# Turning a small side input on VectorE instead of TensorE, in the middle of a feed-forward stage

## The chip, the cores and the metric

The kernel runs on one core of one Trainium2 chip. The metric is the device time of one execution in microseconds (us), the smaller the better. TensorE is written PE, VectorE DVE, ScalarE ACT, GpSimd POOL, SyncE SP. PEld is TensorE's weight load.

## The reference, cut to what matters

Two transformer blocks run one after the other on one sequence of 256 rows with model width 1024, all in float32. The first block ends with a relu-squared feed-forward and a gate fed by the small side input `p` (256 x 256):

```python
h2 = rms_norm(x, g_mlp[i])
x = x + jnp.square(jax.nn.relu(h2 @ w_ff1[i])) @ w_ff2[i]     # 1024 -> 4096 -> 1024

gate_p = jax.nn.sigmoid(rms_norm(x, g_ple[i]) @ w_ple_gate[i])
x = x + gate_p * (p[i] @ w_ple[i])                            # p: 256 x 256, w_ple: 256 x 1024
```

The second block (two gated feed-forwards around an attention stage) follows.

## The kernel before, in words

**Split products.** Each float32 operand is held as a high part (a copy rounded to the type `fp32r`) and a low part (the operand minus its high part). A product is three matmuls: high by high, high by low, low by high. Both weights and activations are split so.

**Units.** The weights come in as *units* of 128 x 2048, in a fixed order written out by hand. SP loads a unit into one of six `raw` buffers, ACT copies it to `w_hi` (line 1034, four buffers; it waits until the unit four before is used up), and DVE subtracts to `w_lo` (`lo`, line 1479), in place of `raw`. For a few units POOL does this subtraction (line 2159). PE waits, at the start of each unit, for `lo_ready` to have counted that unit (`products`, matmuls in line 519). In this stage a unit is 24 matmuls of 512 columns.

**The relu stage.** The width 4096 is cut into eight slices, i = 0 to 7. With ff the number of the stage's first unit, slice i takes two units for the way up (for i > 0, ff+4(i-1) and the one after; slice 1 takes ff+2 and ff+3) and two for the way down. PE's order is up(i), then down(i-2). So for i = 5 PE works on units ff+16 and ff+17 (up), then ff+18 and ff+19 (down of slice 3). For each slice:

- ACT takes the relu of the two PSUM banks into `act_r` (line 1212), DVE makes the square into `act_f` (`square`, line 1740) and frees the banks,
- DVE turns `act_f` into `relu_T` with 16 transposes of 32 x 256 (`relu_turn`, line 1755), which wait for both squares to be finished,
- ACT copies the high part to `fT_hi` or `fE_hi` (line 1216), DVE subtracts the low part (`relu_low`, line 1762).

DVE's order in slice i > 2 is `lo(v+3)`, `relu_low(i-1)`, `lo(v+4)`, the two squares, `relu_turn(i)`, `lo(v+5)`, `lo(v+6)`, with v = ff+4(i-1). All queues run in the order of the program.

**The side input.** POOL loads `p` into `p_sb` ahead of the stage (line 2201). After up(0), PE turns it with four transposes (matmuls with the unit matrix, line 533) into one PSUM bank of the two *work* banks (6 and 7), which serve all such turned batches of the kernel in turn, by each batch's number in one list (`WB`). ACT then copies the bank to `pT_hi` (line 1041) and DVE subtracts to `pT_lo` (line 1498), between the second square and `relu_turn(0)`. The product with `w_ple` uses them at the end of the stage (`ple_product`).

**The idle buffer.** `act_T` (128 x 512) holds turned activations in the two gated feed-forwards of the second block. They fill it with the same sort of 16 transposes, of 32 x 128 (line 1848). In the relu stage it is not used.

Of the kernel before, what the change touches and what calls it, by code (L numbers as in the profile page):

```python
# [28 lines left out]
P = 128  # L29
D, TB, SEQ = 1024, 2, 256  # L30
# [66 lines left out]
def work_batches():  # L97

    order = [("mix", 0, 0), ("mix", 1, 0), ("mix", 0, 1), ("mix", 1, 1)]
    for k in range(IN_CB):  # L100
        if 6 <= k < 14:
            order += [("v", k - 6)]
        if k == IN_CB - 1:
            order += [("ya", 0, 0)]
        if 12 <= k:
            order += [("rv", k - 12)]
    order += [("ya", 0, 1)]
    order += [("ya", 1, h) for h in range(2)]
    order += [("yr", tb, h) for tb in range(TB) for h in range(2)]
    order += [("m", tb, h) for tb in range(TB) for h in range(2)]  # L110
    order += [("mlp", tb, h) for tb in range(TB) for h in range(2)]
    order += [("p",)]
    order += [("ple", tb, h) for tb in range(TB) for h in range(2)]
    order += [("ffn1", tb, h) for tb in range(TB) for h in range(2)]
    order += [("mix2", tb, h) for tb in range(TB) for h in range(2)]
    order += [("cq", 0), ("cq", 1), ("ckv",)]
    for kind in "bl":
        for j in range(BH // 2):
            order += [(kind + "a", 2 * j), (kind + "a", 2 * j + 1)]
            order += [(kind + "v", j)]  # L120
    order += [("ffn2", tb, h) for tb in range(TB) for h in range(2)]
    return {name: n for n, name in enumerate(order)}
# [56 lines left out]
def two_blocks(nc, x_d, p_d, g_mix, w_in, lam_q1, lam_k1, lam_q2, lam_k2, g_diff, g_ret, w_bd, w_br, w_out,  # L179
# [3 lines left out]
    f32, f32r, bf16, i32 = mybir.dt.float32, mybir.dt.float32r, mybir.dt.bfloat16, mybir.dt.int32  # L183
    ALU, ACT = mybir.AluOpType, mybir.ActivationFunctionType
# [51 lines left out]
    def lay(start, *parts):  # L236

        out = []
        for name, shape, *dt in parts:
            out.append(sb(name, shape, dt[0] if dt else f32, start))  # L240
            start += -(-4 * int(np.prod(shape[1:])) // 32) * 32
        assert start <= nc.sbuf_usable_end, (name, start)
        return out
# [15 lines left out]
    fT0, fT1, act_r, act_f, pl_s, sg, pT0, pT1, p_sb, gain_mid, fE0, fE1 = lay(  # L259
        arena, ("fT_hi", [P, 4, SEQ], f32r), ("fT_lo", [P, 4, SEQ], f32r), ("act_r", [P, TB, HALF]),  # L260
        ("act_f", [P, TB, HALF]), ("pl_s", [P, TB, D]), ("sg", [P, TB, D]),
        ("pT_hi", [P, 2, SEQ], f32r), ("pT_lo", [P, 2, SEQ], f32r), ("p_sb", [P, TB, 256]), ("gain_mid", [P, D]),
        ("fE_hi", [P, 4, SEQ], f32r), ("fE_lo", [P, 4, SEQ], f32r))
    fT, pT, fE = [fT0, fT1], [pT0, pT1], [fE0, fE1]
    act_T, relu_T = lay(named["fE_lo"] + 16 * SEQ, ("act_T", [P, 2, SEQ]), ("relu_T", [P, 4, SEQ]))
# [34 lines left out]
    def sem(name):  # L300
        sems[name] = ctx.enter_context(nc.semaphore(name))
        return sems[name]
# [10 lines left out]
    p_in, ident_in, mask_in, lam_in, gd_in = (sem(n) for n in ("p_in", "ident_in", "mask_in", "lam_in", "gd_in"))  # L313
# [15 lines left out]
    proj_done, proj_out = sem("proj_done"), sem("proj_out")  # L329
    qk_turned = sem("qk_turned")  # L330
    acc_done, acc_out = sem("acc_done"), sem("acc_out")
    relu_turned, f_hi, f_ready = sem("relu_turned"), sem("f_hi"), sem("f_ready")
    act_turned, turned_hi, turned_lo = sem("act_turned"), sem("turned_hi"), sem("turned_lo")
    up_done, act_ready, up_out = sem("up_done"), sem("act_ready"), sem("up_out")
# [162 lines left out]
    def _(pe):  # L497
# [25 lines left out]
        def work_free(n, dw=0):  # L523
            if n >= 2:
                pe.wait_ge(work_out[n % 2], n // 2 + dw)

        def turn(name, blocks, dw=0):

            work_free(WB[name], dw)
            col = 0  # L530
            for blk in blocks:
                rows, cols = blk.shape[0], blk.shape[-1]
                mm = pe.transpose(work(name)[0:cols, col:col + rows], blk, ident)  # L533
                col += rows
            mm.then_inc(work_done, 1)

        def turned(name, dw=0):
            n = WB[name]
            pe.wait_ge(work_out[n % 2], n // 2 + 1 + dw)
# [203 lines left out]
        def ff_up0(u0, norm):  # L743

            out = [up(0, 0)[:, :]]
            products(out, hA, 0, 4, 0, u0, HALF, True, False, operand=norm)
            turn_rows(norm, x, 1, (0,))
            products(out, hA, 4, 2, 0, u0 + 1, HALF, False, False, operand=norm)
            turn_rows(norm, x, 1, (1,))
            products(out, hA, 4, 4, 0, u0 + 1, HALF, False, True, t0=2, operand=norm).then_inc(up_done, 1)  # L750
            narrow_block(up(1, 0)[:, :], norm, u0, 1, HALF)
# [13 lines left out]

        u = U0["ff"]
        ff_up0(u, "mlp")
        pe.wait_ge(p_in, 16)
        turn(("p",), [p_sb[:, tb, k * P:(k + 1) * P] for k in range(2) for tb in range(TB)])

        def relu_up(i):

# [32 lines left out]
        def ple_product(tb):  # L805

            if tb:
                pe.wait_ge(pl_out, 1)
            turned(("p",))
            mm = products([bank[4 + c][:, :] for c in range(2)], pT, 0, 2, tb, U0["pl"], D, True, True)  # L810
            mm.then_inc(unit_used if tb else pl_done, 1)

# [208 lines left out]
    def _(act):  # L1021
        def loads(u):

            return 32 * (u // RAW_SLOTS + (u % RAW_SLOTS > 1))

        def hi(u, turns=0):

            if u >= N_UNITS:
                return
            if u >= HI_SLOTS:  # L1030
                act.wait_ge(unit_used, u - HI_SLOTS + 1 + 12 * turns)
            act.wait_ge(raw_in[u % RAW_SLOTS], loads(u) + 64 * turns)
            w = unit_width(u)
            act.activation(w_hi[u % HI_SLOTS][:, 0:w], raw[u % RAW_SLOTS][:, 0:w], ACT.Copy).then_inc(hi_ready, 1)  # L1034

        def split(name, di=0):

            act.wait_ge(work_done, WB[name] + 1 + 2 * di)
            (dst, _), b = rows_of(name)
            if name[0] not in COLUMN:  # L1040
                act.activation(dst, b, ACT.Copy).then_inc(split_hi, 1)
                return
            c0 = COLUMN[name[0]] + BLOCKS * name[2]
            act.wait_ge(g_ready, 1 if name[0] == "mix" else 2)
            for n in range(BLOCKS):
                act.activation(dst[:, n, :], b[:, n, :], ACT.Copy, scale=g_col[:, c0 + n:c0 + n + 1]).then_inc(split_hi, 1)  # L1046
# [171 lines left out]
        relu(0, 0)  # L1218
        hi(U0["ff"] + 4)
        relu(0, 1)  # L1220
        split(("p",))

        hi(U0["ff"] + 5)
        relu_split(0)
# [4 lines left out]
        for i in range(2, DFF // HALF):  # L1229
            v = U0["ff"] + 4 * (i - 1)  # L1230
            hi(v + 3)
            relu_split(i - 1)
            hi(v + 4)
            for tb in range(TB):
                relu(i, tb)
            hi(v + 5)
            hi(v + 6)
# [122 lines left out]
        for n in range(1, 5):  # L1360
# [6 lines left out]
            if n == 2:  # L1367
                act.wait_ge(proj_out, copies(CB_IN2 + 2))
                for tb in range(TB):
                    for m, (buf, cols) in enumerate(((cq, QR), (ckv, KVR))):  # L1370
                        if tb or m:
                            act.wait_ge(csq, 2 * tb + m)
                        k = 2 * m + tb
# [41 lines left out]
        for tb in range(TB):  # L1415
            k = act.activation(k_tm[:, tb, :, NOPE:MQ], kr[:, tb, :].unsqueeze(1).to_broadcast([P, MH, ROPE]), ACT.Copy)
# [47 lines left out]
    def _(vec):  # L1464
# [26 lines left out]
        def split(name, di=0):  # L1491

            if name[0] in COLUMN:
                low_blocks(name, range(BLOCKS))
                return
            (hi, dst), b = rows_of(name)
            vec.wait_ge(split_hi, SPLIT[name] + 1 + 2 * di)
            vec.tensor_tensor(dst, b, hi.bitcast(f32), ALU.subtract).then_inc(work_out[WB[name] % 2], 1)
# [244 lines left out]
        square(0, 0)  # L1743
        lo(U0["ff"] + 4)
        square(0, 1)
        split(("p",))

        def relu_turn(i):

            vec.wait_ge(up_out, 2 * i + 2)  # L1750
            whole = act_f[:, :, :].rearrange("p t (k j f) -> p t k j f", j=4, f=32)
            there = relu_T[:, :, :].rearrange("p k (t a c) -> p t k a c", a=4, c=32)
            for a in range(4):
                for j in range(4):
                    t = vec.transpose(there[32 * j:32 * j + 32, :, :, a, :], whole[32 * a:32 * a + 32, :, :, j, :])  # L1755
            t.then_inc(relu_turned, 1)

        def relu_low(i):

# [12 lines left out]
        for i in range(2, DFF // HALF):  # L1772
            v = U0["ff"] + 4 * (i - 1)
            if i > 2:
                lo(v + 3)
            relu_low(i - 1)
            if i > 2:
                lo(v + 4)
            for tb in range(TB):
                square(i, tb)  # L1780
            if i == 2:
                vec.wait_ge(lo_ready, v + 5)
                lo(v + 5)
            relu_turn(i)
            if i > 2:
                lo(v + 5)
            lo(v + 6)
# [524 lines left out]
```

## Time and profile before

| | |
|---|---|
| median of 3 runs | 966.04 us (965.82 to 966.35) |
| the profiled execution: its own time | 966.08 us |
| its span, first to last instruction | 964.2 us |
| the relu stage in that span | from about 283 to 451 us |

The span counts from the first instruction of the profile. An execution's own time is the span and 1.9 us around it. Starts in the rows below are in us from the span's start; a row of a timeline may hold several instructions one after the other.

### The profile page before, as it was taken

What the parts mean: (1) busy time and instruction counts of PE and PEld (TensorE: products, weight loads), DVE (VectorE), ACT (ScalarE), POOL (GpSimd) and SP (SyncE); (2) the same over time, 40 slices, a digit from 0 to 9 for tenths busy, and PEclk for the clock granted to TensorE, in tenths of its full rate; (3) what the DMA queues carried; (4) which work ended last, traced back from release to release, by engine and by line L of the source; (5) the groups of instructions that cost most, each with busy time, mean ns of one, the idle gap of its engine ahead of it and who ended that gap; (6) DMA issues with size and microseconds to landing.
All of it is one profiled execution on the core that took longest, in us unless ns stands there. A gap on an engine that the chain in (4) does not pass through costs nothing.

```text
span 964.2 us, 12923 instructions
## 1 busy us (share of the span) xinstructions
PE 956.4 (99%) x4468; PEld 786.7 (82%) x4468; DVE 772.1 (80%) x1489; ACT 500.9 (52%) x666; POOL 162.5 (17%) x118
## 2 busy tenths in 40 slices
PE   9999999999999999999999999999999999999997
PEld 6887778888888888888888888888887788888886
DVE  6897997578669799884778987877878878887875
ACT  7545556644463644444765444444648665444442
POOL 3552444310013300000133000000133023000000
PEclk9999999999999999999999999999999999999999
DMA  9865555434455755554566656553654255656531
GB/s 343 269 193 167 165 174 175 150 130 175 175 203 205 240 176 191 202 187 164 172 215 196 213 177 204 187 177 113 223 182 147 88 175 187 206 177 206 184 131 44
DMA packets 98725, 175.67 MB, mean 182 GB/s; under 512 B 5920, under 2 KB 54128, under 8 KB 98672
## 3 DMA queue, kind: packets, MB, share of 16 engines
q1 hardware_dynamic: 97024, 171.53, 53.0%
q0 software_dynamic: 1344, 3.19, 1.2%
q8 instruction: 31, 0.51, 0.2%
q10 hardware_dynamic: 304, 0.27, 0.1%
q14 instruction: 22, 0.18, 0.1%
HBM read 173.91 MB, written 1.05 MB: 181 GB/s over the span
## 4 chain that ended last, share of the span: by engine, by line
PE 93%; DVE 4%; issue 1%; ACT 1%; POOL 1%; DMA 0%; POOLq 0%; ACTq 0%; DVEq 0%
PE bank L519 86%; PE bank L533 2%; DVE relu_T L1755 2%; DVE w_lo L1479 1%; PE bank L578 1%; PE bank L577 1%; PE bank L904 1%; PE bank L589 1%; POOL w_lo L2159 0%; ACT w_hi L1034 0%; PE bank L960 0%; DMA g_rows<-in_g_mix 0%; PE bank L591 0%; PE bank L590 0%; DVE act_f L1740 0%
## 5 line engine op out<-in xcount | busy, mean ns | idle before, releaser
L519 PE MATMUL bank<-w_hi,hA 128*128 128x512 f32 (+1 forms) x1752 | 544.8, 390 | 0.0
L1034 ACT ACTIVATE w_hi<-raw 128x2048 fp32r<-128x2048 f32 (+1 forms) x162 | 305.8, 1893 | 196.7 <-PE bank L519 194.9
L519 PEld LDWEIGHTS bank<-w_hi,hA 128*128 128x128 f32 x1752 | 327.4, 188 | 67.7 <-issue 1.1
L1479 DVE TENSOR_TENSOR w_lo<-raw,w_hi 128x2048 fp32r<-128x2048 f32 (+1 forms) x138 | 308.2, 2254 | 63.1 <-ACT w_hi L1034 58.1
L519 PE MATMUL bank<-w_lo,hA 128*128 128x512 f32 (+1 forms) x876 | 334.3, 388 | 0.0
L519 PEld LDWEIGHTS bank<-w_lo,hA 128*128 128x128 f32 x876 | 164.5, 188 | 33.0
L2159 POOL TENSOR_TENSOR w_lo<-raw,w_hi 128x2048 fp32r<-128x2048 f32 x21 | 96.8, 4609 | 154.5 <-ACT w_hi L1034 121.9
L1848 DVE STREAM_TRANSPOSE act_T<-act_f 32x128 f32<-32x128 f32 x352 | 106.5, 303 | 5.7 <-DVE act_f L1836 0.7
L2145 POOL TENSOR_SCALAR ms<-ss 128x1 f32<-128x1 f32 x15 | 9.8, 654 | 515.9 <-ACT junk L1064 515.6
L519 PE MATMUL bank<-w_hi,fT_hi 128*128 128x512 f32 x232 | 71.5, 389 | 0.0
L519 PE MATMUL bank<-w_hi,fT_lo 128*128 128x512 f32 x232 | 71.4, 389 | 0.0
L519 PE MATMUL bank<-w_lo,fT_hi 128*128 128x512 f32 x232 | 71.4, 389 | 0.0
L1755 DVE STREAM_TRANSPOSE relu_T<-act_f 32x256 f32<-32x256 f32 x128 | 55.8, 436 | 1.9
L519 PEld LDWEIGHTS bank<-w_lo,fT_hi 128*128 128x128 f32 x232 | 43.5, 188 | 9.0
L519 PEld LDWEIGHTS bank<-w_hi,fT_lo 128*128 128x128 f32 x232 | 43.5, 188 | 9.0
L519 PEld LDWEIGHTS bank<-w_hi,fT_hi 128*128 128x128 f32 x232 | 43.5, 188 | 9.0
L1290 ACT ACTIVATE act_r<-bank,rs 128x256 f32<-128x256 f32 x44 | 20.6, 474 | 54.0 <-PE bank L519 52.2
L1506 DVE SCALAR_TENSOR_TENSOR hA<-bank,g_col,hA 128x128 fp32r<-128x128 f32 x92 | 25.3, 344 | 15.6 <-ACT hA L1046 15.4
L1836 DVE SCALAR_TENSOR_TENSOR act_f<-bank,rs,act_r 128x256 f32<-128x256 f32 x44 | 20.8, 480 | 21.2 <-ACT act_r L1290 21.1
L1575 DVE STREAM_TRANSPOSE aT<-L 32x96 f32<-32x96 f32 x128 | 34.5, 270 | 1.9
L1046 ACT ACTIVATE hA<-bank,g_col 128x128 fp32r<-128x128 f32 x92 | 25.5, 378 | 18.2 <-PE bank L533 18.1
L519 PE MATMUL bank<-w_hi,hB_hi 128*128 128x512 f32 x96 | 30.4, 398 | 0.0
(281 smaller groups left out, 906.7 us busy)
## 6 DMA issues: line engine op xcount, KB each, us to landing
raw<-in_w_in SPq DMA_DIRECT2D x74, 512.0 KB, 4.7
raw<-in_w_ff SPq DMA_DIRECT2D x64, 512.0 KB, 4.0
raw<-in_ffn_w_gate SPq DMA_DIRECT2D x44, 512.0 KB, 3.9
raw<-in_ffn_w_up SPq DMA_DIRECT2D x44, 512.0 KB, 4.8
raw<-in_ffn_w_down SPq DMA_DIRECT2D x44, 512.0 KB, 4.0
raw<-in_w_out SPq DMA_DIRECT2D x16, 512.0 KB, 3.8
raw<-in_w_branch_diff SPq DMA_DIRECT2D x8, 512.0 KB, 3.9
raw<-in_w_branch_ret SPq DMA_DIRECT2D x8, 512.0 KB, 3.7
```

What stands on the lines that cost most here:

```text
L519: mm = pe.matmul(o, a, w, start=first and t == 0 and m < len(outs), stop=last and t == n - 1 and m >= len(todo) - len(outs))
L533: mm = pe.transpose(work(name)[0:cols, col:col + rows], blk, ident)
L1034: act.activation(w_hi[u % HI_SLOTS][:, 0:w], raw[u % RAW_SLOTS][:, 0:w], ACT.Copy).then_inc(hi_ready, 1)
L1046: act.activation(dst[:, n, :], b[:, n, :], ACT.Copy, scale=g_col[:, c0 + n:c0 + n + 1]).then_inc(split_hi, 1)
L1290: act.activation(act_r[:, tb, 0:SUB], up(tb, i)[:, 0:SUB], ACT.Silu, scale=inv_rms(norm, tb))\
L1479: vec.tensor_tensor(w_lo[u % RAW_SLOTS][:, 0:w], raw[u % RAW_SLOTS][:, 0:w], w_hi[u % HI_SLOTS][:, 0:w].bitcast(f32), ALU.subtract).then_i ...
L1506: vec.scalar_tensor_tensor(out=dst[:, n, :], in0=b[:, n, :], scalar=g_col[:, c0 + n:c0 + n + 1], in1=hi[:, n, :].bitcast(f32), op0=ALU.mul ...
L1575: t = vec.transpose(there[32 * j:32 * j + 32, :, a, :], whole[32 * a:32 * a + 32, :, j, :])
L1755: t = vec.transpose(there[32 * j:32 * j + 32, :, :, a, :], whole[32 * a:32 * a + 32, :, :, j, :])
L1836: vec.scalar_tensor_tensor(out=act_f[:, tb, 0:SUB], in0=up(tb, i)[:, SUB:2 * SUB], scalar=rs[:, n:n + 1], in1=act_r[:, tb, 0:SUB], op0=ALU ...
L1848: t = vec.transpose(there[32 * j:32 * j + 32, :, :, a, :], whole[32 * a:32 * a + 32, :, :, j, :])
L2159: pool.tensor_tensor(w_lo[u % RAW_SLOTS][:, 0:w], raw[u % RAW_SLOTS][:, 0:w], w_hi[u % HI_SLOTS][:, 0:w].bitcast(f32), ALU.subtract).then_ ...
```

## The change

`p` no longer goes through PE and a work bank. After `relu_turn(4)`, DVE turns `p_sb` into `act_T` with 16 transposes of 32 x 128 (`p_turn`). In slice 5, ACT copies all of `act_T` to `pT_hi` in one instruction, behind its `hi(v + 4)`, and DVE subtracts to `pT_lo` in one instruction, behind `relu_turn(5)`. The batch `p` is gone from the list of work batches, so that each later batch takes the other of the two banks than before. `ple_product` waits for the new semaphore `p_lo`.

```diff
@@ work_batches
-    order += [("p",)]
@@ PE, after ff_up0(u, "mlp")
-        pe.wait_ge(p_in, 16)
-        turn(("p",), [p_sb[:, tb, k * P:(k + 1) * P] for k in range(2) for tb in range(TB)])
@@ PE, ple_product
-            turned(("p",))
+            pe.wait_ge(p_lo, 1)
@@ ACT, after relu(0, 1)
-        split(("p",))
@@ ACT, slices 2 to 7, between hi(v + 4) and relu(i, tb)
+            if i == 5:
+                act.wait_ge(p_turned, 1)
+                act.activation(pT[0][:, :, :], act_T[:, :, :], ACT.Copy).then_inc(p_hi, 1)
@@ DVE, after square(0, 1)
-        split(("p",))
@@ DVE
+        def p_turn():
+
+            vec.wait_ge(p_in, 16)
+            whole = p_sb[:, :, :].rearrange("p t (k j f) -> p t k j f", j=4, f=32)
+            there = act_T[:, :, :].rearrange("p k (t a c) -> p t k a c", a=4, c=32)
+            for a in range(4):
+                for j in range(4):
+                    t = vec.transpose(there[32 * j:32 * j + 32, :, :, a, :], whole[32 * a:32 * a + 32, :, :, j, :])
+            t.then_inc(p_turned, 1)
@@ DVE, slices 2 to 7
             relu_turn(i)
+            if i == 4:
+                p_turn()
+            if i == 5:
+                vec.wait_ge(p_hi, 1)
+                vec.tensor_tensor(pT[1][:, :, :], act_T[:, :, :], pT[0][:, :, :].bitcast(f32), ALU.subtract).then_inc(p_lo, 1)
             if i > 2:
                 lo(v + 5)
             lo(v + 6)
```

## Rows read from the trace of the kernel before

**Rows 1.** The page: span, busy time by engine, granted TensorE clock by slice

```profile
span 964.2 us, 12923 instructions
PE 956.4 (99%) x4468; PEld 786.7 (82%) x4468; DVE 772.1 (80%) x1489; ACT 500.9 (52%) x666; POOL 162.5 (17%) x118
PEclk9999999999999999999999999999999999999999
```

**Rows 2.** The chain that ended last, by time: start, us, what

```profile
292.73 0.60 DVE pT_lo L1498
...
317.11 4.65 POOL w_lo L2159
...
331.19 2.31 DVE w_lo L1479
333.63 122.69 PE bank L519 x540
```

**Rows 3.** Timeline of DVE, 280 to 336 us (start, duration, instruction, idle before)

```profile
292.04 0.69 DVE L1740 SCALAR_TENSOR_TENSOR act_f<-bank,act_r 128x512 f32<-128x512 f32 x1
292.64 0.68 DVE L1498 TENSOR_TENSOR pT_lo<-bank,pT_hi 128x512 fp32r<-128x512 f32 x1
293.24 7.17 DVE L1755 STREAM_TRANSPOSE relu_T<-act_f 32x256 f32<-32x256 f32 x16
...
331.19 4.49 DVE L1479 TENSOR_TENSOR w_lo<-raw,w_hi 128x2048 fp32r<-128x2048 f32 x2
```

**Rows 4.** Timeline of PE: the transposes of p, the wait at 333 us, unit ff+16

```profile
289.26 0.60 PE L533 MATMUL bank<-masks,p_sb 128*128 128x128 f32 x4
289.61 0.48 PE L519 MATMUL bank<-w_hi,hA 128*128 128x512 f32 x1
...
333.04 0.39 PE L519 MATMUL bank<-w_hi,hA 128*128 128x512 f32 x1
333.63 0.70 PE L519 MATMUL bank<-w_hi,fE_hi 128*128 128x512 f32 x2 [0.20 <-DVE w_lo L1479]
...
366.39 0.39 PE L519 MATMUL bank<-w_hi,hA 128*128 128x512 f32 x1
...
377.27 0.61 PE L519 MATMUL bank<-w_hi,fE_hi 128*128 128x512 f32 x2
```

**Rows 5.** Timeline of DVE, 336 to 460 us, slices 4 and 5

```profile
358.73 7.18 DVE L1755 STREAM_TRANSPOSE relu_T<-act_f 32x256 f32<-32x256 f32 x16
365.94 6.70 DVE L1479 TENSOR_TENSOR w_lo<-raw,w_hi 128x2048 fp32r<-128x2048 f32 x3
372.56 1.22 DVE L1762 TENSOR_TENSOR fT_lo<-relu_T,fT_hi 128x1024 fp32r<-128x1024 f32 x1
373.98 2.29 DVE L1479 TENSOR_TENSOR w_lo<-raw,w_hi 128x2048 fp32r<-128x2048 f32 x1 [0.21 <-ACT w_hi L1034]
...
378.10 0.69 DVE L1740 SCALAR_TENSOR_TENSOR act_f<-bank,act_r 128x512 f32<-128x512 f32 x1 [1.23 <-ACT act_r L1212]
378.83 7.18 DVE L1755 STREAM_TRANSPOSE relu_T<-act_f 32x256 f32<-32x256 f32 x16
...
395.74 2.29 DVE L1479 TENSOR_TENSOR w_lo<-raw,w_hi 128x2048 fp32r<-128x2048 f32 x1 [1.87 <-ACT w_hi L1034]
```

**Rows 6.** Timeline of DVE in the second block, one turn into act_T

```profile
503.65 5.04 DVE L1848 STREAM_TRANSPOSE act_T<-act_f 32x128 f32<-32x128 f32 x16
```

**Rows 7.** Instructions that touch act_T (ns min/median/max, first and last start)

```profile
L1295 ACT ACTIVATE fT_hi<-act_T x22: 608/612/637, 508.7 to 948.3; 128x512 fp32r<-128x512 f32 x22
L1855 DVE TENSOR_TENSOR fT_lo<-act_T,fT_hi x22: 682/684/695, 509.4 to 949.0; 128x512 fp32r<-128x512 f32 x22
```

**Rows 8.** Timeline of ACT in slice 5

```profile
372.03 1.92 ACT L1034 ACTIVATE w_hi<-raw 128x2048 fp32r<-128x2048 f32 x1 [2.57 <-PE bank L519]
374.75 0.60 ACT L1212 ACTIVATE act_r<-bank 128x512 f32<-128x512 f32 x1 [0.80 <-PE bank L519]
```

**Rows 9.** A stretch of time: busy (count) by engine, granted clock, DMA share, GB/s

```profile
355.40:377.20 21.80, 21.80 (x98) 18.06 (x97) 21.00 (x25) 9.71 (x7) 0.00 (x0) 1.00 0.54 193
```

More of the change, by code:

```diff
@@ L331, in two_blocks @@
     acc_done, acc_out = sem("acc_done"), sem("acc_out")
+    p_turned, p_hi, p_lo = sem("p_turned"), sem("p_hi"), sem("p_lo")
     relu_turned, f_hi, f_ready = sem("relu_turned"), sem("f_hi"), sem("f_ready")
```

## The prediction

> **What bounds the kernel now.** I read the page first. TensorE is busy for 99% of the span, VectorE for 80%, at full clock in every slice [rows 1]. So a change on another engine matters only where PE waits for it, or where it starts to. Which places those are is told by the chain of waits in order of time: from 333.63 us on it is PE alone for 122.69 us, but the stretch before, from about 284 to 333 us, hangs on DVE, with one link on POOL [rows 2]. One of its DVE links is `pT_lo`, 0.60 us, which the change removes. The timelines then show how close the two engines run: at 333 us PE waits for the low half of unit ff+10 (started by DVE at 331.19) [rows 3, 4], and from there DVE still runs back to back without any idle time until 373.98 [rows 5]; in the stretch from 355.4 to 377.2 it is busy for 21.00 of 21.80 us [rows 9]. Only after that has it room: it idles 0.21 and 1.23 us in slice 5, and 1.87 us ahead of one `lo` in slice 6 [rows 5]. The added 16 transposes stand at 365.94, ahead of this room. That is the place to work out.
>
> **The change part by part.**
>
> *Removed from PE:* four transposes. The next matmul starts 0.35 us after the first of them [rows 4], so PE is up to about 0.4 us earlier from 289 us on. This is worth nothing by itself: PE waits for DVE at 333 us anyway, and would come there 0.4 us earlier to wait longer.
>
> *Removed from ACT:* one copy of 128 x 512, about 0.6 us by the like copy out of `act_T` [rows 7]. ACT is not in the chain there.
>
> *Removed from DVE:* `pT_lo`, from 292.64 to 293.24 before `relu_turn(0)` starts [rows 3]. Not all of its 0.60 us comes back. `relu_turn` waits for the end of the second square. That ends at 292.04 + 0.69 = 292.73 [rows 3]; in slice 5 the turn starts 0.04 us behind such an end (378.10 + 0.69 = 378.79, then 378.83) [rows 5]. So `relu_turn(0)` moves from 293.24 to 292.77: 0.47 us. The chain up to 333 us is DVE, ACT behind it, and POOL behind ACT [rows 2], so all of it moves by 0.47: unit ff+10 is ready at 331.19 + 2.29 - 0.47 = 333.01 (2.29 is one such subtraction, [rows 5]). PE could start it at 333.04 + 0.227 - 0.4 = 332.87, so it still waits, and it too is then 0.47 us ahead. (0.227 us is the step of a matmul: 48 of them between 366.39 and 377.27 [rows 4].) **Term 1: -0.47 us**, for both engines, at 333 us.
>
> *Added to DVE, slice 4:* 16 transposes of 32 x 128. The trace has the same form in the second block: 5.04 us for 16, so 5.05 to the next instruction [rows 6]. Source and strides differ (`p_sb` instead of `act_f`), the count of elements does not. They push what is behind them in DVE's queue: `lo` of ff+17, ff+18 and ff+19, then `relu_low(4)`, `lo` of ff+20, the squares of slice 5. The first is late first. It starts at 365.94 [rows 5]; now 365.94 - 0.47 + 5.05 = 370.52, and ends 2.29 later, at 372.81. PE begins unit ff+16 at 366.39 [rows 4] and so needs ff+17 at 366.39 + 24 x 0.227 = 371.83, now 371.36. From the end of a subtraction to the waiting matmul take 0.15 us (333.48 to 333.63 [rows 3, 4]): PE starts at 372.96. **Term 2: +1.60 us** of new waiting. And a stop costs a little behind it: after the one at 333.63, 144 matmuls take 366.39 - 333.63 = 32.76 us instead of 144 x 0.2267 = 32.64. **Term 3: +0.12 us.** (The stop at 333 us pays this with and without the change.)
>
> Is anything else late? With PE now at 372.96 for ff+17 it needs ff+18 at 378.5 and ff+19 at 384.0. DVE ends them at 375.0 and 377.2, then `relu_low(4)` at 378.4, `lo` of ff+20 at 380.6 (PE: about 389.4), the squares at about 381.9, `relu_turn(5)` at 389.1. The two PSUM banks are free by 381.9, and up(6) wants them at 389.4. No second wait.
>
> *Added in slice 5:* ACT's copy of 0.61 us [rows 7] behind its `hi(v + 4)`, which starts at 372.03 now and ends at 373.95; the next item there waits for PE until 374.75 [rows 8], and PE is 1.25 us later than that in the new order. `p_turn` is done by 370.5. The copy fits that gap; without it the relu of slice 5 would be late by at most 0.6 us. DVE's subtraction of 0.68 us [rows 7], 0.6 to the next, delays `lo` of ff+21 to an end at about 392.0; PE needs it at about 394.9. DVE is then some 2.5 us later against PE than before, and in slice 6 it has 1.87 + 1.23 us of idle time to make it up [rows 5]. Cost: nothing, by that cover of 2.9 us; gone, it would be 0.6.
>
> *The moved wait for p, and the banks:* `p` was in `p_sb` before PE turned it at 289 us [rows 4], so DVE does not wait for it at 365 us. No DMA moves. All later work batches swap between banks 6 and 7; each still waits for the batch two before it in the list, so I cost this at 0, with 0.6 us either way as the bound, the one link of the chain that such a batch has [rows 2].
>
> *Against the skill.* The 16 transposes take 5.04 us on DVE [rows 6], where PE's four take less than half a microsecond of its time [rows 4]. The Trainium skill (VectorE: DVE Perf Modes, Rules for kernel authors) advises TensorE for 128 x 128 transposes if PSUM will do as the destination; this case's rows agree on the direction. Its section "The three transpose paths" gives 311 ns for a 128 x 128 of bf16 on VectorE; an estimate by that page would be 4 x 0.311 = 1.24 us for all of `p`, no new wait, and a sum of term 1 alone, -0.47.
>
> *Sum:* -0.47 + 1.60 + 0.12 = +1.25 us. On the profiled execution's own 966.08 us (0.04 above the median of the runs): **967.3 us**.
>
> *Bounds of the one unknown price:* each microsecond of `p_turn` beyond 3.45 us (371.36 - 365.47 - 2.29 - 0.15) is a microsecond of waiting. From below: 0 us of waiting; from above the dearer form of the turn, 7.18 us for 16 of 32 x 256 [rows 5]. I take the row with the same number of elements.
>
> **The rivals.**
>
> 1. *No new wait.* `p_turn` costs under 3.45 us, or PE comes later to ff+17 than I reckon. Only term 1 is left: -0.47, 965.6 us. Against it stands the row of 5.04 us. The skill's figure above is of this side.
> 2. *A dearer turn: slower.* If the two strided rows of `p_sb` cost like the 32 x 256 form, 7.20 us, DVE delivers ff+17 another 2.15 us later: 969.5 us. It decides from a `p_turn` of 5.73 us up (1.93 us above before). Against it: the row of 5.04 us is of the same shape, 32 partitions of 2 x 2 x 32 elements, with strided rows at both ends too.
> 3. *The saving is lost.* POOL's link at 317 us or another release holds the chain where it was, so term 1 is 0. Then ff+17 is late by the same distance from before's clock: +1.72, 967.8 us. For it: one link of the chain is POOL's [rows 2]; against: POOL starts only when ACT, itself behind DVE's turn, has made the high half.
> 4. *The clock falls in the new stop.* Against it: the page shows the highest digit of the granted clock in every slice, that of the wait at 333 us among them [rows 1], and 1.00 just behind it [rows 9]. For it: that stop was 0.4 us (333.27 to 333.63 [rows 4]) and this is 1.6. If unit ff+17 ran at 1.2 GHz instead of 2.4, its 24 matmuls would take 5.44 us more: 972.8 us.
>
> **How the numbers follow.** My forecast has 0.66, rival 1 0.11, rival 2 0.08, rival 3 0.08, rival 4 0.03, and 0.04 stay for effects of the new banks and program that I can't place, half to each side. A change of 0.2%, 1.93 us, is about what a measurement of this kernel can tell from none. The forecast, rival 1 and rival 3 lie within it, less 0.02 to 0.04 at their edges. Slower: 0.08 + 0.03 + 0.02 + 0.04 = 0.17. Faster: 0.02 + 0.02 = 0.04. Same: 0.79. The range from 965.0 to 968.6 takes in rivals 1 and 3 with the banks' 0.6 us, and half of the way to rival 2. The forecast's own range is 966.7 to 967.9.
>
> **What would show it.** In the trace after: `relu_turn(0)` starts 0.47 us earlier than it did; PE's wait at 333 us is still there, some 0.3 us; the 16 transposes take 5.04 us and start near 365.5; one new wait of PE, 1.6 us long, at 371.4 for `w_lo`, with PE's matmuls at 372.96; no other wait up to the end of the stage; granted clock at 1.00. The prediction is wrong if `p_turn` has another price, if PE comes to ff+17 at another time, or if a second wait follows.

## The result and the profile after

| | before | after |
|---|---|---|
| median of 21 runs each | 965.96 us (965.49 to 966.63) | 967.53 us (967.05 to 968.74) |
| ratio, 95% interval | | 1.0016 (1.0009 to 1.0022) |
| profiled execution: own time, span | 966.08, 964.2 us | 967.52, 965.7 us |
| stage time (below) | 182.34 us | 183.55 us |

The changed kernel is 0.16% slower, a loss of 1.57 us by the medians. That lies inside the 0.2% that I had called no change, but the interval of the ratio does not hold 1: with 21 runs the small loss can be told. The forecast was 967.3 us, with 966.7 to 967.9 as its own range.

The span's start differs by some tenths of a microsecond between executions, so I compare a stretch with the same work of PE at both ends: from the start of the group of eight transposes just ahead of the stage to the start of the one just behind it. I call its length the **stage time**. In the chain of waits of the kernel before, those two rows are

```profile
273.98 0.87 PE bank L533 x8
...
456.32 0.87 PE bank L533 x8
```

and in that of the changed kernel

```profile
273.84 0.87 PE bank L533 x8
...
370.42 2.30 DVE w_lo L1479
372.76 84.62 PE bank L519 x372
457.39 0.87 PE bank L533 x8
```

So the stage takes 457.39 - 273.84 = 183.55 us instead of 456.32 - 273.98 = 182.34: 1.21 us more, where the sum had 1.25. The chain shows the place too: before, PE set the pace from 333.63 us on [rows 2]; now DVE does so up to 372.76, by the low half of a unit (`w_lo`).

The timeline of DVE after, for [rows 3] and [rows 5]:

```profile
284.70 4.49 DVE L1479 TENSOR_TENSOR w_lo<-raw,w_hi 128x2048 fp32r<-128x2048 f32 x2
...
291.90 0.69 DVE L1740 SCALAR_TENSOR_TENSOR act_f<-bank,act_r 128x512 f32<-128x512 f32 x1
292.62 7.18 DVE L1754 STREAM_TRANSPOSE relu_T<-act_f 32x256 f32<-32x256 f32 x16
...
365.34 5.05 DVE L1764 STREAM_TRANSPOSE act_T<-p_sb 32x128 f32<-32x128 f32 x16
370.42 6.70 DVE L1479 TENSOR_TENSOR w_lo<-raw,w_hi 128x2048 fp32r<-128x2048 f32 x3
377.03 1.22 DVE L1771 TENSOR_TENSOR fT_lo<-relu_T,fT_hi 128x1024 fp32r<-128x1024 f32 x1
378.17 2.29 DVE L1479 TENSOR_TENSOR w_lo<-raw,w_hi 128x2048 fp32r<-128x2048 f32 x1
380.37 1.28 DVE L1740 SCALAR_TENSOR_TENSOR act_f<-bank,act_r 128x512 f32<-128x512 f32 x2
381.69 7.18 DVE L1754 STREAM_TRANSPOSE relu_T<-act_f 32x256 f32<-32x256 f32 x16
388.90 0.69 DVE L1798 TENSOR_TENSOR pT_lo<-act_T,pT_hi 128x512 fp32r<-128x512 f32 x1
389.51 6.69 DVE L1479 TENSOR_TENSOR w_lo<-raw,w_hi 128x2048 fp32r<-128x2048 f32 x3
```

`relu_turn(0)` now follows the second square by 0.72 us instead of 1.20 [rows 3]; the turn of `p` takes 5.05 us; and from 365.34 on there is no idle time between these rows, where before there were 0.21 and 1.23 us in slice 5 [rows 5]. The timeline of PE after, for [rows 4]:

```profile
332.41 0.39 PE L519 MATMUL bank<-w_hi,hA 128*128 128x512 f32 x1
333.02 0.69 PE L519 MATMUL bank<-w_hi,fE_hi 128*128 128x512 f32 x2 [0.23 <-DVE w_lo L1479]
...
370.98 0.39 PE L519 MATMUL bank<-w_hi,hA 128*128 128x512 f32 x1
372.76 0.50 PE L519 MATMUL bank<-w_hi,hA 128*128 128x512 f32 x1 [1.40 <-DVE w_lo L1479]
...
378.34 0.62 PE L519 MATMUL bank<-w_hi,fE_hi 128*128 128x512 f32 x2
```

The matmul at 370.98 is the last of ff+16. The next could have started 0.227 us later, at 371.21; it starts at 372.76. The bracket counts the stop from the modelled end of the matmul before, the steps from start to start: 1.55 us lost. From 372.76 to 378.34 the 24 matmuls of ff+17 take 5.58 us, 0.14 more than 24 x 0.2267. ACT's copy falls where it was put, in the gap behind `hi(v + 4)`:

```profile
371.40 1.91 ACT L1032 ACTIVATE w_hi<-raw 128x2048 fp32r<-128x2048 f32 x1 [2.58 <-PE bank L519]
373.22 0.61 ACT L1233 ACTIVATE pT_hi<-act_T 128x512 fp32r<-128x512 f32 x1
375.82 0.60 ACT L1210 ACTIVATE act_r<-bank 128x512 f32<-128x512 f32 x1 [1.99 <-PE bank L519]
```

### The profile page after: what moved, and what is told of

Read it like the earlier page. It is cut to its first block, busy times and chain, and to the rows that moved or that the text cites. A ratio compares the mean times of both kernels' runs of the same rounds, so it can differ in the third digit from the quotient of the medians.

```text
span 965.7 us, 12930 instructions
## 1 busy us (share of the span) xinstructions
PE 956.2 (99%) x4464; PEld 786.2 (81%) x4464; DVE 776.8 (80%) x1505; ACT 500.9 (52%) x666; POOL 162.5 (17%) x118
## 4 chain that ended last, share of the span: by engine, by line
PE 87%; DVE 8%; DMA 1%; ACT 1%; issue 1%; POOL 1%; SPq 1%; POOLq 0%; ACTq 0%; DVEq 0%
PE bank L519 81%; DVE relu_T L1754 4%; DVE w_lo L1479 3%; PE bank L533 2%; DMA raw<-in_w_in 1%; PE bank L578 1%; PE bank L577 1%; ACT w_hi L1032 1%; PE bank L902 1%; PE bank L589 1%; DVE act_f L1740 1%; DVE act_T L1764 1%; POOL w_lo L2173 0%; PE bank L958 0%; PE bank L591 0%
```

## The experiments

Each is an edit of the changed kernel, except where the kernel before is named. Ratios are to the kernel before, run on the same chip; the stage time is from each profile, start of the one group of eight transposes to start of the other. Each has 11 runs, except `half_each` with 10, `twice` with 4 and the changed kernel with 21. The medians of before that they stand beside are 965.96 us (changed kernel, `half_each`, `low_late`, `twice`, `both_moved`), 966.05 (`behind_lo`, `slice5`, `copy_only`, `bank_kept`) and 966.02 (`three_moved`, `spare_turn`).

| run | stage time | against before | median | ratio, 95% interval |
|---|---|---|---|---|
| changed kernel | 183.55 | +1.21 | 967.53 | 1.0016 (1.0009 to 1.0022) |
| behind_lo | 181.86 | -0.48 | 965.84 | 0.9999 (0.9990 to 1.0008) |
| slice5 | 181.89 | -0.45 | 965.77 | 0.9997 (0.9988 to 1.0006) |
| half_each | 181.86 | -0.48 | 965.87 | 1.0001 (0.9992 to 1.0010) |
| copy_only | 181.87 | -0.47 | 965.43 | 0.9994 (0.9985 to 1.0003) |
| low_late | 181.86 | -0.48 | 965.60 | 0.9996 (0.9987 to 1.0005) |
| twice | 190.19 | +7.85 | 974.43 | 1.0087 (1.0071 to 1.0102) |
| bank_kept | 183.57 | +1.23 | 967.58 | 1.0018 (1.0009 to 1.0027) |
| both_moved | 181.76 | -0.58 | 965.78 | 0.9998 (0.9989 to 1.0007) |
| three_moved | 181.36 | -0.98 | 965.42 | 0.9996 (0.9987 to 1.0005) |
| spare_turn | 182.34 | 0.00 | 966.23 | 1.0003 (0.9994 to 1.0012) |

Most intervals of the ratios are about 0.1% wide to each side, 0.9 us. They tell the changed kernel, `bank_kept` and `twice` from before, and no more. The stage times, one profiled execution each, tell the others apart: five kernels without the wait at 371 us agree within 0.03 us. Three of them have the turn on DVE in other places, one has a copy in its stead, and in one PE still turns `p`.

### behind_lo: the same turn behind two low halves

```diff
             relu_turn(i)
-            if i == 4:
-                p_turn()
...
             lo(v + 6)
+            if i == 4:
+                p_turn()
```

> The same 16 transposes of p on VectorE, in the same slice 4, but behind the low halves of units ff+17 and ff+18 instead of in front of them. Theory (the whole loss is TensorE's wait for ff+17): the wait at 371 us is gone, ff+17 is ready at 367.8, ff+19 at 377.2 where TensorE needs it at 382.2; only the 0.47 us of the chain before 333 us remain: ratio to before 0.9995, about 965.5 us. Rival (the 16 transposes cost time wherever they stand, or the swapped banks do): the time stays at about 967.3 to 967.5. Rival (term 1 is lost outside the profile): 965.9 to 966.0.

The same 16 transposes, in the same slice:

```profile
365.48 4.49 DVE L1479 TENSOR_TENSOR w_lo<-raw,w_hi 128x2048 fp32r<-128x2048 f32 x2
369.89 5.04 DVE L1764 STREAM_TRANSPOSE act_T<-p_sb 32x128 f32<-32x128 f32 x16
374.96 2.29 DVE L1479 TENSOR_TENSOR w_lo<-raw,w_hi 128x2048 fp32r<-128x2048 f32 x1
```

They cost as much of DVE's time as before (5.04 us) and nothing of the stage's: 181.86 us, 1.69 less than in the changed kernel, which is terms 2 and 3 (1.72). So the loss belongs to the order of the queue and not to the work, and -0.48 is term 1 by itself. The median moved by 0.21 us, less than the 0.48; see the open point at the end of the next section.

### slice5: in front of its low half, one slice later

```diff
-            if i == 4:
+            if i == 5:
                 p_turn()
-            if i == 5:
+            if i == 6:
                 vec.wait_ge(p_hi, 1)
```

(and ACT's wait and copy in slice 6.)

> The turn one slice later, still in front of its lo(v+5): behind relu_turn(5), with the two splits of p in slice 6. VectorE has 1.4 us of idle time more against TensorE there, which has room of about 3.1 us in a slice. Theory: ff+21 is ready at 385.6 + 5.05 + 2.3 = 392.9, and TensorE needs it at 393.1: no wait or one under 0.2 us; 965.5 us (965.4 to 965.8). Rival (a price by the transposes' number): 967.3 to 967.5.

181.89 us: no wait at ff+21 in the timeline of PE. DVE there:

```profile
384.98 5.05 DVE L1764 STREAM_TRANSPOSE act_T<-p_sb 32x128 f32<-32x128 f32 x16
390.07 6.70 DVE L1479 TENSOR_TENSOR w_lo<-raw,w_hi 128x2048 fp32r<-128x2048 f32 x3
```

PE begins ff+20 at 387.10, so it comes to ff+21 at 387.10 + 24 x 0.2267 = 392.54; the low half is done at 390.07 + 2.29 = 392.36, just in time. In slice 4 DVE had 3.45 us in front of PE at this place, one slice later just over 5. The gain is 1.66 us: in the kernel before, DVE goes from this place in slice 4 (365.94) to the same place in slice 5 (386.04) in 20.10 us, and PE takes 96 x 0.2267 = 21.76 us for the four units of a slice.

### half_each: eight in front, eight behind

```diff
+            if i == 4:
+                p_turn(range(2))
...
             lo(v + 6)
+            if i == 4:
+                p_turn(range(2, 4))
```

> Eight of the 16 transposes stand in front of the low half of ff+17 as in the change, eight behind that of ff+18. Theory: the first eight take 2.52 us, under the 3.45 us that VectorE has there; no wait at 371 us, and the stage (between 274 and 456 us) takes 181.87 us, 0.47 less than before. Rival (a turn in front of ff+17 costs by its length from the first microsecond on): half of the change's loss, the stage at 182.7.

181.86 us. 2.51 us of transposes in front of ff+17 cost nothing, 5.05 cost 1.55: the price of work at this place is not proportional to its length, it is what exceeds the room.

### copy_only: no turn at all

```diff
-            for a in range(4):
-                for j in range(4):
-                    t = vec.transpose(there[32 * j:32 * j + 32, :, :, a, :], whole[32 * a:32 * a + 32, :, :, j, :])
-            t.then_inc(p_turned, 1)
+            vec.tensor_copy(act_T[:, :, :], p_sb[:, :, :]).then_inc(p_turned, 1)
```

> The 16 transposes are left out: one plain copy of p into act_T takes their place, so p goes in unturned and the output is not the reference's. All else is as in the changed kernel: the banks, the two splits, the removal on TensorE. Theory: the copy takes about 0.4 to 0.7 us, under the 3.45 us that VectorE has, so no wait at 371 us; only the 0.47 us gained remain: 965.5 us. Rival (banks, code or the late splits cost 0.3 us or more): 965.8 to 966.3. If the extra 0.3 us of the changed kernel's runs over my sum comes from those, it shows here too.

181.87 us, the same as with the turn in a place with room.

### low_late: the kernel before, with pT_lo moved

```diff
         square(0, 1)
-        split(("p",))
...
             relu_turn(i)
+            if i == 5:
+                split(("p",))
```

> The kernel before with one edit: VectorE's subtraction to pT_lo stands behind relu_turn(5) instead of in front of relu_turn(0). TensorE still turns p, and no transposes are added. Theory: VectorE gains the same 0.47 us before 333 us, which makes ff+10 ready about when TensorE comes to it (333.16 against 333.27): its stop there goes, 0.36 us and what it costs behind, and the stage is 0.47 us shorter: ratio 0.9995, 965.5 us. Rival (TensorE's own 0.4 us of transposes is on the path too): the stage shortens by less than 0.3 us.

181.86 us, and no wait of PE on a low half is left in the stage. The gain comes from moving one subtraction out of DVE's chain; to have it, `p` need not be turned on DVE. That it is again 0.48 is partly chance: here PE itself, which still turns `p`, sets the limit, and what goes is its stop of 0.36 us and the 0.12 behind it. In `behind_lo` PE still stops at 333 us, and the gain is what DVE's chain moved by.

### twice: the turn two times in front of ff+17

```diff
+            spare = sg[:, 0, 0:512].rearrange("p (k t a c) -> p t k a c", k=2, a=4, c=32)
+            for dst in (spare, there):
-            for a in range(4):
+                for a in range(4):
```

> The 16 transposes of p stand there twice, the first set into a buffer that nobody reads: 32 instead of 16, in front of the low half of ff+17. Theory: each microsecond of the turn is one of waiting, so TensorE's stop at 371 us grows by 5.05 us: ratio 1.0069, 972.3 to 972.7 us; between 274 and 456 us of the profile TensorE needs 5.05 us more than in the changed kernel's (183.55 there). Rival (the granted clock falls after the longer stop of some 6.7 us): matmuls of 512 columns at a step of 0.453 us instead of 0.227 for some time behind it, the slice of the page under its highest digit, and a microsecond or more above 972.7. Rival (the wait isn't the turn's): less than 5 us more.

The stage takes 6.64 us more than in the changed kernel, and the median of 974.43 us lies above the 972.3 to 972.7 of the theory. 5.05 us of the 6.64 are the second turn. The other 1.59 are the first rival's, the fall of the clock. The timeline of PE, and busy time with the granted clock (the number behind the five engines) in stretches:

```profile
371.67 0.39 PE L519 MATMUL bank<-w_hi,hA 128*128 128x512 f32 x1
378.51 0.79 PE L519 MATMUL bank<-w_hi,hA 128*128 128x512 f32 x1 [6.45 <-DVE w_lo L1479]
379.10 0.63 PE L519 MATMUL bank<-w_lo,hA 128*128 128x512 f32 x1
379.53 1.05 PE L519 MATMUL bank<-w_hi,hA 128*128 128x512 f32 x2
380.38 0.63 PE L519 MATMUL bank<-w_lo,hA 128*128 128x512 f32 x1
```

```profile
340.00:371.00 31.00, 31.00 (x139) 25.67 (x138) 30.25 (x56) 14.05 (x10) 0.00 (x0) 1.00 0.59 200
371.00:378.00 7.00, 1.06 (x5) 0.56 (x3) 6.75 (x18) 2.54 (x2) 0.00 (x0) 0.79 0.45 164
378.00:381.00 3.00, 2.49 (x6) 2.01 (x7) 3.00 (x3) 0.00 (x0) 0.00 (x0) 0.50 0.00 0
381.00:384.00 3.00, 3.00 (x13) 2.42 (x12) 3.00 (x3) 0.60 (x1) 0.00 (x0) 0.85 0.00 0
384.00:390.00 6.00, 6.00 (x29) 4.95 (x28) 5.90 (x9) 2.40 (x2) 0.00 (x0) 1.00 0.48 173
```

During a stop of 6.6 us (371.90 to 378.51) the granted clock fell to 0.50, the level of 1.2 GHz, and it was back at 1.00 by 384 us. At the lower level the matmuls started 0.43 us after one another instead of 0.227. From the start at 378.51 to that of the matmul at 384.08, 17 steps took 5.57 us instead of 17 x 0.2267 = 3.85. The 1.72 us lost there are the 1.59 and the 0.14 that the changed kernel loses behind its stop too. The Trainium skill (TensorE: Matmul & The Clock Gate, What's actually happening) gives these two levels and ties them to how busy the array was; this trace agrees.

### bank_kept: the work batches in their old banks

```diff
-    work = lambda name: bank[6 + WB[name] % 2]
+    work = lambda name: bank[6 + (WB[name] + (WB[name] > WB["mlp", 1, 1])) % 2]
```

> The changed kernel, but each work batch behind the relu stage is put back into the bank of 6 and 7 that it had in the kernel before. Theory: banks are worth nothing, the time is that of the changed kernel, 967.3 to 967.6. Rival (the swapped banks cost the 0.3 us by which the changed kernel's runs lie above my sum): 967.1 to 967.2.

183.57 us and a median of 967.58. In the stretch behind the stage, where the banks differ, the profile has 496.72 us from the second group of eight transposes to the first `x` of the last stage, against 496.69 in the changed kernel: the banks are worth nothing that a profile shows.

### both_moved and three_moved: after PE's 0.4 us

`behind_lo` still has PE's wait at 333 us, so the four transposes saved on PE bring nothing. `both_moved` takes ff+10 in front of `relu_turn(2)`, and the turn of `p` behind the two low halves:

```diff
             if i == 2:
                 vec.wait_ge(lo_ready, v + 5)
                 lo(v + 5)
+                lo(v + 6)
             relu_turn(i)
-            if i == 4:
-                p_turn()
...
             if i > 2:
                 lo(v + 5)
-            lo(v + 6)
+                lo(v + 6)
+            if i == 4:
+                p_turn()
```

> A version meant to beat both: the turn of p behind the low halves of ff+17 and ff+18, and in slice 2 the low half of ff+10 made in front of relu_turn(2) instead of behind it. Theory: the last wait of TensorE in the stage, at 333 us, goes (ff+10 is ready at about 325.5), and TensorE keeps also the 0.44 us of the four transposes: the stage takes 0.36 + 0.12 + 0.44 = 0.92 us less than before, 181.4 us; ratio 0.9990, 965.1 us. Rival (relu_turn(2), 2.2 us later, makes something else late, such as the high half of ff+12 behind ACT's copy): another wait in its place, and a stage of 181.9 or more.

The wait at 333 us went, but only 0.58 us came, not 0.92. The rest is in the timeline of PE at 349 us, by the step from one start to the next:

```profile
348.96 0.97 PE L519 MATMUL bank<-w_hi,hA 128*128 128x512 f32 x2
349.76 0.40 PE L519 MATMUL bank<-w_lo,hA 128*128 128x512 f32 x1
```

Two matmuls in 0.80 us instead of 0.45, just where unit ff+13 begins, whose low half started on DVE at 347.08 and took 2.29, to 349.37. PE wanted it at 348.96 + 0.227 = 349.19. So the next unit was late, and the stop and the restart behind it cost 0.35 us together. This is what the rival feared, at another unit than it named and for less: 181.76 us lie between the theory's 181.4 and the rival's 181.9. `three_moved` puts `lo(v + 5)` in front of `relu_turn(i)` in slices 3 and 4 as well (the edit against `both_moved`):

```diff
+            if i in (3, 4):
+                lo(v + 5)
             relu_turn(i)
-            if i > 2:
+            if i > 4:
                 lo(v + 5)
+            if i > 2:
                 lo(v + 6)
```

> As both_moved, and in slices 3 and 4 too the low half of the next unit to go up (ff+13, ff+17) is made in front of relu_turn instead of behind it. Theory: what kept both_moved at 0.58 us instead of 0.92 is that ff+13 was next to be late, by 0.3 us at 349 us; with its subtraction 7.2 us earlier no wait is left in the stage: 181.4 us between 274 and 456 us, 0.92 less than before; ratio 0.9990 to 0.9993. Rival (something behind the later relu_turn(3) is late in its turn, as ff+13 was): 181.6 or more.

181.36 us, 0.98 less than before, and no wait of PE on DVE in the whole stage. Its median of 965.42 us was 0.60 below that of before beside it (966.02), but the interval of the ratio holds 1. It beats the changed kernel, since the intervals of the two ratios do not meet (this one ends at 1.0005, the other begins at 1.0009), and the kernel before only by the profile.

### spare_turn: the kernel before with 16 idle transposes

```diff
             lo(v + 6)
+            if i == 5:
+                p_turn()
```

(with `p_turn` as in the change, its result unused.)

> The kernel before, with 16 transposes of p into act_T added, that nobody reads, behind the low half of ff+22 in slice 5, where VectorE has room. Theory: no wait comes of them, the stage stays at 182.34 us and the time at that of before, 965.8 to 966.2 us. Rival (instructions added to VectorE cost some 0.3 us outside the stage, as the medians of the kernels with the turn seem to say): 966.3.

The stage stays at 182.34 us to the last digit. The median lies 0.21 us above that of before, between the two expectations.

## Why the prediction was right

**Term 1, -0.47 us.** `relu_turn(0)` started 0.62 us earlier, 0.14 of it because that whole execution ran 0.14 us earlier (284.84 became 284.70 for DVE's first row of the stretch). That is 0.48. `copy_only` and `behind_lo` have it without the wait at 371 us: -0.47 and -0.48. `low_late` shows that it needs only the subtraction moved, though its -0.48 is PE's limit (see there). That the 0.60 us of the instruction bring only 0.47, since the next instruction waits for an end and not for the queue, was right. Rival 3 is ruled out.

**Term 2, +1.60 us.** 1.55 us measured. The price of the turn was right to 0.01 us (5.05), so rival 2 had no room; `half_each` and `behind_lo` show that a turn inside the room makes rival 1's time, so 3.45 us of room was of the right order. Two small errors of the sum went against each other. The next subtraction started 5.08 us behind the start of the turn (365.34 to 370.42) and not 5.05. And from its end at 372.72 to the waiting matmul at 372.76 it was 0.04 us, not the 0.15 that I had carried over from the stop at 333 us. The Trainium skill has a figure for a transpose of 128 x 128 in bf16 on VectorE (VectorE: DVE Perf Modes, The three transpose paths); the estimate from it was 1.24 us for all of `p`. The measurement here, 5.05 us for four such blocks of f32, decides.

**Term 3, +0.12 us.** 0.14 measured behind the stop.

**What I costed at nothing.** No second wait followed, ACT's copy fell in its gap, DVE made up its delay by slice 6, and the banks were free (`bank_kept`). In slice 6 after the change, DVE waits for ACT's relu again before the second square, 0.79 us, and the turn that follows starts at 401.66. In the kernel before, this turn started at 400.59. It is 1.07 us later, as much as the end of the stage (456.32 to 457.39): DVE is no further behind PE than before.

**Rival 4.** It did not come: in the 5.5 us behind the stop of 1.55 us the granted clock stood at 1.00.

```profile
372.80:378.30 5.50, 5.50 (x24) 4.57 (x25) 5.50 (x4) 1.63 (x3) 0.00 (x0) 1.00 0.48 174
```

`twice` shows that it was a fair rival for a longer stop; its price there was 1.59 us, not the 5.44 that I gave for a whole unit at half speed. The row that I cited for the clock just behind the wait at 333 us [rows 9] is one of 355.4 to 377.2. The row of the right place says the same:

```profile
333.40:355.40 22.00, 21.80 (x97) 18.05 (x97) 21.73 (x27) 10.86 (x9) 0.00 (x0) 1.00 0.55 191
```

**What stays open.** The medians are 1.57 us apart, the stage times 1.21. The forecast's +1.25 is right for the stage and 0.32 short of the medians. That 967.3 still lies only 0.23 below the measured 967.53 is a little luck: it was added to 966.08, which is 0.12 above the median of before over 21 runs. The kernels that turn `p` on DVE (`behind_lo`, `slice5`, `half_each`, `bank_kept`, `both_moved`, `three_moved`, `twice`) have medians 0.2 to 0.6 us above what their stage times say, `spare_turn` 0.2, `low_late` and `copy_only`, without it, 0.1 above and 0.15 below. The stretch behind the stage is the same in all (from 456.32 to the first `x` at 953.06 it is 496.74 us before, 496.69 after, 496.71 in `behind_lo`), so any such cost would lie at the start or the end of the program. Ahead of the stage the profiles differ by up to 1.1 us (its first group of transposes starts at 273.41 to 274.52) with no order in it. The very end gives a hint. From the end of the last DMA issue of the output to the end of the span it is 2.64 us in the kernel before and 3.11 after. In the other kernels it is 2.65 and 2.69 in the two without the 16 transposes of `p` (`low_late`, `copy_only`), 2.82 to 3.11 in eight with them (the changed kernel among them), but 2.68 in `twice`, which has the most. This is one execution each, and nothing here says why the last transfer should take longer. All of these differences are inside the intervals; whether some tenths belong to added instructions, I can't say.

## What to carry to other kernels

When work moves from a full engine to one that runs just ahead of it, don't price it by its length. Find the next thing behind it in the queue that the full engine waits for, and subtract the room in front of that: here 5.05 us of work in a place with about 3.5 cost 1.55 us, and 0.14 for the restart, and two instructions further down the queue it cost the stage nothing. And a gain on the full engine (here four transposes, 0.4 us) comes through only once every later hand-over has room for it: here it took three moved subtractions to collect it.

## What was not expected of the hardware

A restart of the matmul stream after a stop cost 0.12 to 0.14 us beyond the stop itself, also when the stop was 0.36 us. And a wait of 6.6 us in the middle of a full stream was enough for the granted clock to fall, at a price of 1.59 us more, while stops of 0.36 and 1.55 us left it at 1.00.
